# A streamed expert layer: experts taken in pairs, a hand-written ending, and loads between the layers moved

## The reference, cut to what matters

```python
g_logits = (xt @ w_group + b_group); grp = argmax(g_logits)          # one of 8 groups for each token
top_val, top_idx = top_k(e_logits_of_that_group, 2)                    # two of its 8 experts
comb = softmax(top_val) * p_grp
h = silu(xb @ w1[e]) * (xb @ w3[e])                                    # for each expert e and its tokens
y = segment_sum((h @ w2[e]) * weight)                                  # x = x + y
```

## Time and profile before

| what | value |
|---|---|
| median of 3 runs | 1919.57 us (1918.85 to 1920.22) |
| profiled execution, its own time | 1920.6 us |
| its span, first to last instruction | 1918.7 us |
| TensorE busy | 1881.6 us (98%) |
| VectorE busy | 1436.6 us (75%) |
| ScalarE busy | 1218.7 us (64%) |
| mean granted TensorE clock, share of full | 0.993 |

### The profile page before, as it was taken

The page is one execution under the profiler, slowest core; times in us unless marked ns, Lnnn a source line. Parts: engine busy times, 40 slices in busy tenths (PEclk is TensorE's granted clock), DMA queues, the critical chain, the costliest instruction groups (busy, mean ns, idle before and its releaser), DMA issues.

```text
span 1918.7 us, 27064 instructions
## 1 busy us (share of the span) xinstructions
PE 1881.6 (98%) x9252; PEld 1567.4 (82%) x9252; DVE 1436.6 (75%) x1838; ACT 1218.7 (64%) x1538; POOL 161.2 (8%) x169
## 2 busy tenths in 40 slices
PE   9999999999999999999999999999999999999997
PEld 7988878888888888888789788788888888888886
DVE  5465545589899899999834655464898999999897
ACT  5465534367777777777635555434677777777775
POOL 1000000120011011010000000002210110110000
PEclk9999999999999999999999999999999999999999
DMA  5221273499999999999612223925999999999992
GB/s 174 73 67 46 81 234 110 166 354 400 386 380 370 380 386 368 382 387 374 217 74 59 66 67 84 232 95 193 378 395 380 393 365 376 389 375 374 385 381 102
DMA packets 158791, 503.54 MB, mean 262 GB/s; under 512 B 22410, under 2 KB 38794, under 8 KB 158704
## 3 DMA queue, kind: packets, MB, share of 16 engines
q1 hardware_dynamic: 146192, 459.70, 64.5%
q0 software_dynamic: 12512, 42.69, 7.2%
HBM read 490.18 MB, written 32.79 MB: 273 GB/s over the span
## 4 chain that ended last, share of the span: by engine, by line
PE 91%; DVE 4%; issue 2%; ACT 1%; DMA 1%; DVEq 0%; SPq 0%; POOL 0%; ACTq 0%; POOLq 0%
PE ps L1660 26%; PE ps L1662 26%; PE ps L1661 26%; PE ps L1906 3%; PE ps L1841 2%; PE ps L1890 2%; PE ps L2036 1%; DVE wl L1127 1%; PE ps L1997 1%; PE ps L1951 1%; PE ps L2009 1%; PE ps L1707 1%; DVE gb L1419 1%; DVE ml L1182 1%; PE ps L1836 0%
## 5 line engine op out<-in xcount | busy, mean ns | idle before, releaser
L1127 DVE TENSOR_TENSOR wl<-raw,wh 128x2048 fp32r<-128x2048 f32 (+1 forms) x402 | 908.1, 2278 | 154.7 <-ACT wh L729 152.5
L729 ACT ACTIVATE wh<-raw 128x2048 fp32r<-128x2048 f32 (+1 forms) x406 | 754.2, 1884 | 64.6 <-PE ps L1662 64.0
L1660 PE MATMUL ps<-wh,xgh 128*128 128x512 f32 x1024 | 412.3, 403 | 0.1
L1662 PE MATMUL ps<-wh,xgl 128*128 128x512 f32 x1024 | 400.1, 391 | 0.0
L1661 PE MATMUL ps<-wl,xgh 128*128 128x512 f32 x1024 | 399.2, 390 | 0.0
L1662 PEld LDWEIGHTS ps<-wh,xgl 128*128 128x128 f32 x1024 | 192.2, 188 | 41.6
L1660 PEld LDWEIGHTS ps<-wh,xgh 128*128 128x128 f32 x1024 | 192.3, 188 | 37.5 <-issue 2.2
L1661 PEld LDWEIGHTS ps<-wl,xgh 128*128 128x128 f32 x1024 | 192.9, 188 | 36.0
L1660 PE MATMUL ps<-wh,hth 128*128 128x512 f32 x512 | 200.2, 391 | 2.3 <-DVE htl L1182 2.3
L1662 PE MATMUL ps<-wh,htl 128*128 128x512 f32 x512 | 199.9, 390 | 0.0
L1661 PE MATMUL ps<-wl,hth 128*128 128x512 f32 x512 | 199.4, 389 | 0.0
(11 more groups left out here) (320 smaller groups left out, 2643.4 us busy)
## 6 DMA issues: line engine op xcount, KB each, us to landing
raw<-in_w SPq DMA_DIRECT2D x512, 512.0 KB, 6.1
raw<-in_w SPq DMA_DIRECT2D x128, 1024.0 KB
raw<-in_w_gate SPq DMA_DIRECT2D x16, 1024.0 KB
xslots<-zrow POOLq DMA_DIRECT2D x2, 6240.0 KB, 35.8
raw<-in_w_out SPq DMA_DIRECT2D x8, 1024.0 KB
xg<-xslots POOLq DMA_DIRECT2D x14, 520.0 KB, 7.1
raw<-in_w_in SPq DMA_DIRECT2D x8, 800.0 KB
raw<-in_w_oa SPq DMA_DIRECT2D x4, 1024.0 KB
```

The source lines that it names most:

```text
L729: return nc.scalar.activation(dst, src, ACT.Copy)
L1127: return V.tensor_tensor(dst, src, hi.bitcast(F32), ALU.subtract)
L1660: MM(dst, lh, rh, start=first, stop=False)
L1662: return MM(dst, ll, rh, start=False, stop=last)
```

## The change

Experts are taken in pairs. `FIRST` is now four up units of a pair and then the two downs of the pair before, and so on; `NEXT` has both tail units (experts 6 and 7 of the block before) behind its first four units. Two experts are turned in one group of four transposes, evacuated by one instruction on each engine (`hth_of`, `ht_of`). The first pair is turned behind unit 5, the others behind the second down of a pair. The last block (`FINAL`) ends with a list of its own (`ENDING`), in which the last up unit stands two downs earlier and experts 6 and 7 are turned singly. There VectorE is one unit ahead in the last six units in place of three. `earlier_rows` goes from units 8, 11, 14 and 17 of the last block to units 12, 15, 18 and 21. `yb` is filled behind the second tail unit, unit 5, in place of unit 1. The rows of the next block are turned behind the fourth down. Between the layers the three dense loads, and so the saving of `xl` behind them, wait until the first turned rows of layer 1 are there (`h1_ps`).

```diff
+    def ups(e):
+        return [("up", x, half) for x in (e, e + 1) for half in range(2)]
+    def downs(e, kind="down"):
+        return [(kind, x, 0) for x in (e, e + 1)]
+    FIRST, NEXT = ups(0), ups(0) + downs(NE - 2, "tail")
+    for e in range(2, NE, 2):
+        FIRST += ups(e) + downs(e - 2)
+        NEXT += ups(e) + downs(e - 2)
+    ENDING = [("up", NE - 2, 0), ("up", NE - 2, 1), ("up", NE - 1, 0), ("down", NE - 4, 0), ("up", NE - 1, 1),
+              ("down", NE - 3, 0)] + downs(NE - 2)
+    ALONE = FIRST[:-6] + ENDING
+    FINAL = NEXT[:-6] + ENDING
+    def turned_after(u, units):
+        kind, e, half = u
+        if kind == "tail":
+            return [0, 1] if e == NE - 1 else []
+        if u == ("up", 2, 1):
+            return [0, 1] if units[5] == u else []
+        if units[-1] == ("down", NE - 1, 0) and e >= NE - 3:
+            return {("up", NE - 1, 1): [NE - 2], ("down", NE - 3, 0): [NE - 1]}.get(u, [])
+        return [e + 1, e + 2] if kind == "down" and e % 2 else []
...
-        def in_step(split, units, n0, r, prepared, prepare, at_step, first=None):
+        def in_step(split, units, n0, r, prepared, prepare, at_step, first=None, near=False):
...
-                upto = min(i + AHEAD + 1, len(units) + (AHEAD if prepare else 0))
+                ahead = 1 if near and i >= len(units) - 6 else AHEAD
+                upto = min(i + ahead + 1, len(units) + (AHEAD if prepare else 0))
...
-                        sp.wait_ge(S["used_m"], n_blocks * NU)
+                        sp.wait_ge(S["h1_ps"], 1)
...
-                act.wait_ge(S["used_m"], b * NU + (NU + 1))
+                act.wait_ge(S["used_m"], b * NU + (NU + 4))
...
-                        if kind == "up" and 3 <= e < 3 + NT and half == 0 and prepared and not prepare:
-                            earlier_rows(e - 3)
+                        if n - n0 in (12, 15, 18, 21) and prepared and not prepare:
+                            earlier_rows((n - n0 - 12) // 3)
...
-                    def turn(e):
-                        pe.wait_ge(S["hw_done"], b * NE + (e + 1 + BASE["hw_done"]))
-                        pe.wait_ge(S["htl_done"], b * NE + (e + BASE["htl_done"]))
-                        for j in range(FE // P):
-                            last = nc.tensor.transpose(ps[2][:, j * P:(j + 1) * P], hw[:, e % 2, j * P:(j + 1) * P],
-                                                       ident[:, :])
-                        last.then_inc(S["ht_ps"], 1)
+                    def turn(experts):
+                        pe.wait_ge(S["hw_done"], b * NE + (experts[-1] + 1 + BASE["hw_done"]))
+                        pe.wait_ge(S["htl_done"], b * NE + (experts[0] + BASE["htl_done"]))
+                        for e in experts:
+                            for j in range(FE // P):
+                                at = (e % 2 * (FE // P) + j) * P
+                                last = nc.tensor.transpose(ps[2][:, at:at + P], hw[:, e % 2, j * P:(j + 1) * P],
+                                                           ident[:, :])
+                        last.then_inc(S["ht_ps"], len(experts))
...
-                        if u == ("up", NE - 3, 1) and prepare:
+                        if u == ("down", NE - 5, 0) and prepare:
                             rows_turned(b + 1)
```

More of the change, by code:

```diff
@@ L350, in kv_ready, with hth_of, ht_of @@
                 eng.wait_ge(S["unit_used"], U_QKV[1])
+        def hth_of(experts, part=hth):
+            return part[:, experts[0] % 2:experts[0] % 2 + len(experts), :, :].rearrange("p e k t -> p (e k t)")
+        def ht_of(experts):
+            at = experts[0] % 2 * FE
+            return ps[2][:, at:at + len(experts) * FE]
         def dist_of(t):
@@ L546, in load_units @@
                         else:
-                            ex = (tail_g if kind == "tail" and i < 2 else g) * NE + e
+                            ex = (tail_g if kind == "tail" else g) * NE + e
                             src = w2[l].rearrange("e (k p) n -> e p k n", p=P)
@@ L1019, in step @@
                         kind, e, half = u
[L1020 to L1024, removed]
+                        turned = turned_after(u, units)
+                        if turned:
+                            act.wait_ge(S["ht_ps"], b * NE + (turned[-1] + 1))
+                            nc.scalar.activation(hth_of(turned), ht_of(turned), ACT.Copy
+                                                 ).then_inc(S["hth_done"], len(turned))
                         if kind == "up" and half == 1:
@@ L1036, in step @@
                             nc.scalar.activation(selt[:, :], ps[7][:, :], ACT.Copy).then_inc(S["selt_done"], 1)
-                        if kind == "tail" and n < n0 + 2:
+                        if u == ("tail", NE - 1, 0):
                             y_first(b - 1)
@@ L1611, in step @@
                             selection()
-                        if kind == "up" and 3 <= e < 3 + NT and half == 0 and prepared and not prepare:
-                            earlier_rows(e - 3)
-                        if kind == "tail" and n < n0 + 2:
+                        if n - n0 in (12, 15, 18, 21) and prepared and not prepare:
+                            earlier_rows((n - n0 - 12) // 3)
+                        if u == ("tail", NE - 1, 0):
                             y_second(b - 1)
-                    in_step(lo_unit, units, n0, r, prepared, prepare, step, 1 if isinstance(b, int) and b == 0 else None)
+                    in_step(lo_unit, units, n0, r, prepared, prepare, step, 1 if isinstance(b, int) and b == 0 else None,
+                            near=not prepare)
                 n_blocks = chained_blocks(dve, dve_block, y_added)
@@ L2057, in pe_block @@
                         else:
-                            down(n0 + i, e, kind == "down" or i >= 2)
+                            down(n0 + i, e, kind == "down")
                         if u == ("up", 0, 0) and isinstance(b, int) and b == 0:
@@ L2065, in pe_block @@
                             last.then_inc(S["slot_ps"], 1)
-                        if u in turn_after:
-                            turn(turn_after[u])
-                        if u == ("up", NE - 3, 1) and prepare:
+                        if turned_after(u, units):
+                            turn(turned_after(u, units))
+                        if u == ("down", NE - 5, 0) and prepare:
                             rows_turned(b + 1)
-                        if u == ("up", 3, 0) and not prepare:
+                        if u == ("up", 4, 0) and not prepare:
                             pe.wait_ge(S["sel_made"], (b - (NG - 2)) * NT)
```

34 lines of the change are left out of this document (11 added, 23 removed).

## The result

The changed kernel takes 1911.28 us (median of 5, 1909.05 to 1912.52), the kernel before beside it 1920.09 (1918.85 to 1921.98): ratio 0.9946, 95% interval 0.9936 to 0.9957. The profiled spans are 1909.3 and 1918.7 us.

A forecast was written before the change was run, and what follows sets the result against it. TensorE, busy 1881.6 of 1918.7 us, was taken as the bound, so only its waits count. Terms 1.0 + 0.9 + 0.6 + 1.0 + 0.9 = 4.4 us gave a median of 1915.2 us, 8-in-10 range 1911.5 to 1921.5.

The forecast's parts named there:

- turn of expert 0 in the loop: Blocks inside the loop: the 0.08 us stall at expert 0's turn goes in 6 blocks of each layer, 1.0 us.
- first block, two layers: First block of each layer: stall of 0.3 us at unit 3 in place of 0.75 at the turn, 0.9 us together.
- 60 groups fewer: Merged turns of four transposes save 0.01 to 0.02 us of change-over per group: 0.6 us (0 to 1.2).
- ends: Last block of each layer: stalls of 1.3 against 1.77 us and 0.7 against 1.27, together 1.0 us gained.
- loads between the layers: Dense loads delayed until layer 1's first turned rows shorten the 5.80 us gap by 0.9 us (0 to 4.3).
- All the other turns run at 0.69 us: Claim that turns outside the listed stalls, first block, expert 0 and last block, lose nothing on TensorE.
- Part 3: Delaying three 0.8 MB loads between the layers, priced by a slowed instruction fetch: 0.9 us, ceiling 4.3.
- Rival 3: Gap between the layers is instruction fetch behind the loads: 3.4 us more gain, 1911.8 us, chance 0.10.
- The gap's length after: Between the layers: layer 1's first turning matmul below 5 us behind the layer's last product, against 5.80 before.
- Rivals 1 and 2: Last added-row read long in layer 0: 1918.6 us, chance 0.17; added rows hold VectorE in both layers: 1922.6 to 1925, 0.14.
- rival 4: The waits only move and the gap between layers stays: 1.6 us gain, 1918 us, chance 0.14.
- What I costed at nothing: Next block's rows fetched 4 units (11 us) later, and the delayed dense loads still landing in time: no stall.

The follow-up runs named there:

- single turns: Changed kernel with each expert turned by itself, eight groups of two transposes a block in place of four of four: 1914.27 us, ratio 0.9964.
- pairs alone: Changed kernel with the later dense loads between the layers undone: 1916.84 us, ratio 0.9978 to the kernel before.
- the loads alone: Kernel before with only the dense loads between the layers made to wait for the first turned rows: 1916.51 us, ratio 0.9981.
- the kernel with two reads: Changed kernel with added rows read into two places in turn and VectorE three units ahead to the end: 1910.73 us, ratio 0.9946.

## Why the prediction was wrong

The sign and most places were right; the time was not, since the sum had a term far too small, lacked another, and came near the truth between the layers only because two errors cancel there. By its steps, in us of the profile:

| step | forecast | measured | from |
|---|---|---|---|
| turn of expert 0 in the loop | 1.0 | 0.8 | 12 x 0.07, gone after |
| first block, two layers | 0.9 | 0.6 | 0.75 to 0.43 |
| 60 groups fewer | 0.6 (0 to 1.2) | 3.9 | 0.063 x 62, single turns |
| ends | 1.0 | -0.1 | 1.77 to 2.1, 1.27 to 1.05 |
| loads between the layers | 0.9 (0 to 4.3) | 4.2 | pairs alone against the changed kernel |
| the pairs' effect on that gap | 0 | -3.2 | 5.80 to 9.01 |
| turn at the loop's edge | none | 2.3 | (0.28 + 0.24) x 6 - 0.8 |
| low-clock stretch at 276 us, untouched code | none | 1.1 | 401.8 to 400.6 |

They add up to 9.6, the profile has 9.4. Against the forecast's 4.4 the groups bring 3.3 more, the loop's edge 2.3 and the low-clock stretch 1.1, while the ends bring 1.1 less; the two rows on the gap together are the forecast's 0.9 within 0.1, and the rest is small. The edge summed turn by turn, ten of them, gives 2.5.

- *The step that failed* is the term "some 60 groups fewer: 0.6 us (0 to 1.2)", from "0.01 to 0.02 us belong to the change-over". It was worked out from the starts about one turn, and the price lies mostly in the nine after them: the runs show 0.063 us a group, 3.9 in all. Its bounds came from the same starts and didn't hold it. The nine starts behind that very turn run at the plain rate, which is the exception in the kernel before: behind most of its turns they take 0.03 to 0.05 us more.
- *"All the other turns run at 0.69 us"* was wrong at the last turn of each block from which the loop goes back, and so the sum lacked 2.3 us. A look at the stretch that holds the loop's branch, or the sum of a block against its parts, would have shown it: 288 matmuls at 0.2265, 16 transposes at 0.109 and 0.87 make 67.85 us, 0.77 short of the 68.62 of the chain, where I had listed stalls of 0.08. Eight groups at some 0.056 beyond their transposes (the mean over the undisturbed turns), 0.24 at the edge and 0.07 at expert 0 make 0.76 of it.
- *Part 3* was priced by the fetch's duration (1.6 against 0.9 us) alone. Its start was 2.7 us late as well, and that is the larger part. The ceiling of 4.3 held, though by little and on another gap than it was meant for (9.01 to 4.82). Rival 3, at 0.10, named the mechanism, which the loads alone show: 2.8 of the 5.8 us. That its 1911.8 is nearest to the measured time is luck, since the groups and the edge brought that, and not the gap. The Trainium skill ("Runtime: NRT & Kernel Launch", Instruction fetch mechanics) has a taken branch to a target outside the fetched pages wait for a fetch of that page. The traces fit this in part: in the changed kernel and in the pairs alone TensorE resumes 1.4 to 1.5 us behind a fetch's end, with the loads alone and the single turns it doesn't wait for the second fetch. They add that a fetch begins 2.5 to 2.7 us later behind the loads.
- *The gap's length after* (below 5 us, forecast) came out at 4.82 by two errors that cancel.
- *The ends*: of the places that were named, unit 23 has its wait, 1.5 us in layer 0 where 0.5 was walked, and the down unit of expert 6 has one in layer 1 alone; that of expert 7, called in time, waits in both layers. The last read of layer 0 took 5.0 us, between the two cases (3.7 and 7.1), and with VectorE one unit ahead its wait fell on two units and not one. Rivals 1 and 2, the long read, came in neither layer (5.0 and 3.9 us), nor did rival 4. The Trainium skill ("DMA: Bandwidth & Descriptors", Anatomy of one DMA) gives 2.0 us plus the bytes over 436 GB/s, by my estimate 3.2 us for this read. It would have landed at 931.3 and held the add for 0.9 us; the trace has 5.0 and 2.74 us, so the measurement decides against it again.
- What I costed at nothing was nothing: `rows_turned` waits for no rows, and ScalarE and VectorE wait for none of the three delayed loads.
- 1.1 us of the profile's gain isn't the change's. The same code before the experts shows a granted clock of 0.77 before and 0.89 after in the mean over 270 to 285 us, and executions of one kernel differ there: the two profiles of the kernel with two reads have 0.77 and 0.89.

## What to carry to other kernels

Before costing an order of work, add a block up from its parts at their plain rates and chase what is left; the stalls without a releaser, at a branch and behind a small group, only show in such a sum, and 0.06 us counted 62 times here. A wait that is met just in time isn't free if a branch back follows it: one unit between `hw` and its turn left 0.38 us of lead and lost time, two left 2.75 us and lost none. Keep large loads away from places where an engine jumps over much code: here they delayed the instruction fetch, and with the longer idle time more of what followed ran at the low clock.

## What the hardware showed that I had not expected

- Behind a group of transposes the next nine or so 128x512 matmuls start every 0.231 to 0.232 us in place of 0.227, whether the group has two (the single turns) or four (the changed kernel); in the kernel before it is 0.227 to 0.232.
- A loop's branch back hides behind about 1.1 us of queued work on TensorE (an estimate); with 0.83 and 0.89 us 0.28 and 0.18 were lost, and the same turn with the same lead lost at most 0.04 on the way into the loop and out of it.
- A 16 KB instruction fetch took 0.9 to 1.6 us, but behind 2.4 MB of queued loads and the saving of `xl` it began 2.7 us later (2.5 in the changed order).
- Two 512 KB reads in flight under the weight stream took 7.7 and 9.7 us, one alone 6.7 to 7.7 in the changed kernel and up to 8.7 in the pairs alone. The Trainium skill ("DMA: Bandwidth & Descriptors", Anatomy of one DMA) has a rule without a term for the load, which gives 3.2 us for this size, an estimate; with the engines quiet the traces have 3.7 to 3.9.
